# Moving chunk loads, splits and conditioning rows around inside one long transformer kernel

## What is computed

```
sh1, sc1, g1, sh2, sc2, g2 = split(silu(c) @ w_mod + b_mod, 6)      # and the same for c_ctx
hc = modulate(rmsnorm(ctx, norm1_g), csh1, csc1)                    # 256 context tokens
k_c, v_c = context_kv(hc)                                           # columns of w_in
hx = modulate(rmsnorm(x, norm1_g), sh1, sc1)                        # 512 tokens
q, k, v, u, ga, gc = split(hx @ w_in)
y_att  = attend(q, [k, k_c], [v, v_c]) @ w_attn_o
y_conv = silu(layernorm(conv31(a * sigmoid(b)) + conv_b)) @ w_conv_o
x = x + g1 * ((sigmoid(ga) * y_att + sigmoid(gc) * y_conv) @ w_out)
```

## Time and profile before

| | us |
|---|---|
| median of 3 runs | 2408.93 |
| lowest, highest | 2408.12, 2412.94 |
| the profiled execution | 2405.39 |
| its span in the trace | 2403.6 |

### The profile page before, as it was taken

How to read it: one execution, slowest core, us unless ns; L and a number is a source line. 1 busy time by engine, 2 the same in 40 slices (tenths; PEclk the granted TensorE clock), 3 DMA queues, 4 the chain that set the end, 5 groups by cost and what they waited for, 6 DMA issues and landing times.

```text
span 2403.6 us, 29853 instructions
## 1 busy us (share of the span) xinstructions
PE 2179.4 (91%) x10645; PEld 1862.9 (78%) x10645; DVE 1769.7 (74%) x3593; ACT 947.4 (39%) x1543; POOL 1002.4 (42%) x647
## 2 busy tenths in 40 slices
PE   3898899887989999899899999999999979998778
PEld 2686677655768999899788898889888867766557
DVE  7874788876451999999788788887888787444552
ACT  3334555424243444354334333333333343443441
POOL 2441222123434665599644344544455524311111
PEclk8899999988999999999999999999999999977779
DMA  7221111153642454456999999999999943211111
GB/s 290 80 70 66 62 50 70 54 178 130 225 140 82 161 166 149 140 204 235 334 346 376 353 337 332 356 348 344 344 340 359 340 168 101 72 35 35 35 36 44
DMA packets 176946, 455.84 MB, mean 190 GB/s; under 512 B 13600, under 2 KB 80544, under 8 KB 175136
## 3 DMA queue, kind: packets, MB, share of 16 engines
q1 hardware_dynamic: 136720, 293.55, 35.5%
q0 software_dynamic: 36864, 134.23, 14.9%
q10 hardware_dynamic: 3216, 26.15, 2.9%
HBM read 409.84 MB, written 44.04 MB: 189 GB/s over the span
## 4 chain that ended last, share of the span: by engine, by line
PE 63%; DVE 24%; ACT 4%; issue 3%; DMA 2%; POOL 1%; SPq 0%; ACTq 0%; DVEq 0%; POOLq 0%
PE bank L652 12%; PE bank L653 12%; PE bank L654 12%; PE bank L957 7%; PE bank L959 7%; PE bank L961 7%; DVE cout L1850 4%; DVE ohB L2135 4%; PE bank L1027 2%; DVE ohA L2134 2%; PE bank L1056 1%; DVE wk L2036 1%; DVE eqb L2086 1%; PE bank L1039 1%; PE bank L773 1%
## 5 line engine op out<-in xcount | busy, mean ns | idle before, releaser
L1561 POOL TENSOR_TENSOR Rl<-raw,Rh 128x1024 fp32r<-128x1024 f32 x179 | 463.6, 2596 | 831.6 <-ACT Rh L1095 831.2
L652 PE MATMUL bank<-XAh,Rh 128*128 128x384 f32 (+1 forms) x1472 | 534.0, 363 | 36.0 <-POOL Rl L1561 15.3
L1095 ACT ACTIVATE Rh<-raw 128x1024 fp32r<-128x1024 f32 x380 | 400.2, 1057 | 323.9 <-PE bank L961 117.0
L654 PE MATMUL bank<-XAh,Rl 128*128 128x384 f32 (+1 forms) x1472 | 519.7, 353 | 0.0
L653 PE MATMUL bank<-XAl,Rh 128*128 128x384 f32 (+1 forms) x1472 | 519.5, 353 | 0.0
L652 PEld LDWEIGHTS bank<-XAh,Rh 128*128 128x128 f32 x1472 | 278.8, 189 | 59.1 <-issue 20.6
L653 PEld LDWEIGHTS bank<-XAl,Rh 128*128 128x128 f32 x1472 | 279.1, 190 | 17.9
L654 PEld LDWEIGHTS bank<-XAh,Rl 128*128 128x128 f32 x1472 | 278.2, 189 | 18.6
L1607 POOL DMA_INDIRECT ga<-in_v,eid x128 | 196.9, 1538 | 197.5 <-DVE y L2197 178.6
L1607 POOL DMA_INDIRECT ga<-in_un,eid x128 | 172.2, 1345 | 217.3 <-DVE act L2189 193.8
L957 PE MATMUL bank<-Rh,XGh 128*128 128x512 f32 x768 | 238.1, 391 | 5.1 <-issue 5.1
(11 more groups left out here) (272 smaller groups left out, 3411.5 us busy)
## 6 DMA issues: line engine op xcount, KB each, us to landing
raw<-in_u SPq DMA_DIRECT2D x128, 512.0 KB
raw<-in_v SPq DMA_DIRECT2D x128, 512.0 KB
wd<-wb ACTq DMA_DIRECT2D x12, 2048.0 KB, 7.4
wg<-wd SPq DMA_DIRECT2D x30, 768.0 KB
raw<-in_w_mod SPq DMA_DIRECT2D x32, 512.0 KB
raw<-in_w_in SPq DMA_DIRECT2D x32, 512.0 KB
gd<-pk SPq DMA_DIRECT2D x64, 192.0 KB, 1.9
gt<-gd SPq DMA_DIRECT2D x16, 768.0 KB, 10.7
```

Source lines behind the costliest of these rows:

```text
L652: e.matmul(o, sh, mh, start=first, stop=False)
L654: return e.matmul(o, sl, mh, start=False, stop=last)
L1095: e.activation(Rh[:, r % NRING, :], raw[:, n % NRAW, :], ACT.Copy).then_inc(s["hi"], 1)
L1561: e.tensor_tensor(Rl[:, r % NRING, :], raw[:, n % NRAW, :], Rh[:, r % NRING, :].bitcast(F32), ALU.subtract).then_inc(s["lo"], 1)
```

## The change

At the start: the squares of ctx are taken in the middle of `high("hx")`, before block 3, and their products go to the second row of `crow`; SP's last `w_mod` load waits only for the squares of x, and the load of `crow`'s second row waits for all six. ACT and POOL split chunk 8 as well as chunk 7 before they turn to `hc`.

At the merge: SP reads back `sga`, then loads the stream up to chunk 59, and only then reads back `sgc`. ACT splits `w_ao` 2 before the sigmoids of `sga`, and all of `w_ao` 3 to 7 before the squares. PE runs `w_ao` 0 to 5 before the mean (in banks 0, 1, 2, 3, 6, 7), `w_ao` 6 before the variance, 7 after it. DVE puts the products with the gate 0 and 1 among the taps (after 12 and 22), and mod rows 20 and 21 too; rows 22 and 23 go into the scaling loop after its second block, rows 24 and 25 with the bias behind that loop.

```diff
@@ psum_plan
     use(("mu",), 4)
-    use(("ao", 0), 0)
-    use(("ao", 1), 1)
     use(("var",), 5, 1, 0)
-    for cb in range(2, 8):
-        use(("ao", cb), cb % 4)
+    for cb in range(8):
+        use(("ao", cb), (0, 1, 2, 3, 6, 7, 0, 1)[cb])
@@ sync_program
                     if k == 7 and i == 1:
-                        e.wait_ge(s["ssq"], 6)
+                        e.wait_ge(s["ssq"], 4)
...
+            e.wait_ge(s["ssq"], 6)
             e.dma_start(crow[:, 1, :], a["crow"][1].partition_broadcast(128)).then_inc(s["crow1"], 16)
...
-            for v, name, lo in ((sga, "sga", 0), (sgc, "sgc", 8)):
-                if lo == 0:
-                    for i in range(3):
-                        e.wait_ge(s[f"pkg{i}"], 16 * PKG.count(i))
-                    e.wait_ge(free[7], USES["y", 31].done)
-                e.dma_start(v[:, :, :], gg[lo:lo + 8].rearrange("m p t -> p m t")).then_inc(s[name], 16)
+            loads(CH["w_ao", 1] + 1)
+            for i in range(3):
+                e.wait_ge(s[f"pkg{i}"], 16 * PKG.count(i))
+            e.wait_ge(free[7], USES["y", 31].done)
+            e.dma_start(sga[:, :, :], gg[0:8].rearrange("m p t -> p m t")).then_inc(s["sga"], 16)
+            loads(CH["w_ao", 7] + 1)
+            e.dma_start(sgc[:, :, :], gg[8:16].rearrange("m p t -> p m t")).then_inc(s["sgc"], 16)
             loads(CH["w_o", 2])
@@ tensor_program
-            for cb in range(4):
+            for cb in range(6):
                 merge_att(cb)
             o, done = hold(("mu",))
...
-            merge_att(4)
-            merge_att(5)
+            merge_att(6)
             o, _ = hold(("var",))
...
-            merge_att(6)
             merge_att(7)
@@ scalar_program
+                    if name == "hx" and k == 3:
+                        square_sums("ctx", cs, 4, 2, crow[:, 1, :])
...
-            square_sums("ctx", cs, 4, 2)
             high("hx", XA, 0, 512, tmps1, {0: 1, 5: 3})
...
-            ahead(CH["w_qkv", 1, 1] + 2)
+            ahead(CH["w_qkv", 2, 0])
             high("hc", XB, 0, 256, tmps)
...
+            ahead(CH["w_ao", 2])
             e.wait_ge(s["sga"], 16)
             for m in range(8):
                 e.activation(sga[:, m, :], sga[:, m, :], ACT.Sigmoid).then_inc(s["sgas"], 1)
-            ahead(CH["w_ao", 1] + 4)
-            for cb in range(2, 5):
-                ahead(CH["w_ao", cb] + 4)
+            ahead(CH["w_ao", 7])
             for cb in range(8):
                 e.wait_ge(s["sub"], cb + 1)
...
-            ahead(CH["w_ao", 7])
             root("conv", rsd[:, :])
@@ gpsimd_program
             low("hx", XA, 0, 512, tmps1, {1: 1})
-            lows(CH["w_qkv", 1, 1] + 2)
+            lows(CH["w_qkv", 2, 0])
             low("hc", XB, 0, 256, tmps)
@@ vector_program
-            for i in range(2):
+            for i in range(3):
                 modulation(16 + 2 * i, 18 + 2 * i)
-                while n_taps < 7 * 31 + (15, 31)[i]:
+                while n_taps < 7 * 31 + (12, 22, 31)[i]:
                     tap()
-            merge_att(0)
-            modulation(20, 22)
-            merge_att(1)
-            merge_att(2)
+                merge_att(i)
...
             merge_att(3)
-            modulation(22, 24)
-            e.wait_ge(s["wmod"], 8)
-            t_mod = mod_bias(16, 24, 0, n_own)
-            modulation(24, 26)
             merge_att(4)
-            merge_att(5)
             u = USES["var",]
             e.wait_ge(s["ltv"], 8)
             variance("conv", rsd[:, :], bank[u.bank][:, :], D)
+            merge_att(5)
...
+                    if cb == 1:
+                        modulation(22, 24)
                     if cb in (3, 7):
                         merge_att(6 + cb // 4)
+            modulation(24, 26)
+            e.wait_ge(s["wmod"], 8)
+            t_mod = mod_bias(16, 24, 0, n_own)
```

## The result

| | kernel before | changed kernel |
|---|---|---|
| runs | 4 | 4 |
| median us | 2410.40 | 2394.24 |
| lowest, highest | 2408.12, 2412.94 | 2386.53, 2395.22 |
| the profiled execution | 2405.39 | 2386.53 |
| its span | 2403.6 | 2384.7 |

The ratio is 0.9926, with a 95% interval of 0.9902 to 0.995: 12 to 24 us faster, where 18.4 were forecast; the medians differ by 16.2. The two spans differ by 18.9. The profiled execution after is the fastest of its four; the kernel as a whole stands nearer to 2394.

The account below looks back on a forecast made before the run. PE, busy 91% of the span, was taken as the bound, so time is won only where it stands still. 9.1 at the start plus 9.3 at the merge, 18.4 us, gave 2390.5 from 2408.93; range 2385 to 2401.

Parts of the forecast that it names:

- Chunk 8: At the start: PE's 8.07 us wait for chunk 8's low half goes, and the slow clock behind it; gain 9.1 us.
- the 1.4 of slow clock: At the start, from 108 to 113: PE's clock of 0.67 behind the wait goes too, 1.4 us.
- The squares: At the start: squaring ctx before block 3 of hx was booked at nothing, 1.5 us either way.
- Up to the mean: In the merge: DVE's taps end 2.7 us later, but the differences start where they did before.
- the price per split: In the merge: each POOL split that falls among DVE's taps costs DVE 2.0 us.
- Mean to reciprocal: In the merge: one projection before the variance and no row transfer in DVE's way; reciprocal 11.6 us sooner.
- Scaling loop: In the merge, behind the reciprocal: two mod rows added to the loop cost 2.3 us.
- Net of the merge: At the scaling loop's end and PE's start of w_co: 9.3 us gained, bounds 7.5 to 11.3.
- The gate on time: Merge; the rival had w_ao 2 landing late, sigmoids and taps slipping 5.3 us: 2395.8 us, chance 0.14.
- The start's gain is not taken back: Before attention; the rival had ACT's roots and norms take it back, only the merge counting: 2399.6 us, chance 0.09.
- The third: Rival, start and merge: equal waits replace both, at chunk 9 or before the variance; 2408.9 us, chance 0.06.
- The fourth: Rival, w_co 1 to 7: loads behind later mod rows make PE wait before seven chunks; 2413.9 us at least, chance 0.05.

Follow-up runs that it names:

- e4: The changed kernel run again, unedited: 2392.95 us, ratio 0.9935 to the kernel before.
- e3: The kernel before with all of the change's merge edits and none at the start: ratio 0.9964 to the kernel before.
- e5: The kernel before with one line moved, so that ACT splits w_ao 7 ahead of the squares: ratio 0.9967 to the kernel before.
- e7: The changed kernel with sgc read back directly behind sga again, the stream behind both: ratio 0.9941 to the kernel before.
- e2: The kernel before with only the squares of ctx moved before block 3 of hx, and SP's waits with them: ratio 1.0007 to the kernel before.
- e6: The changed kernel with w_ao 7 split behind the squares again: ratio 0.9897 to the kernel before.
- e9: The changed kernel with mod rows 22 to 25 and their bias back in front of the variance: ratio 0.9931 to the kernel before.
- e1: The kernel before with only chunk 8 split right behind chunk 7: ratio 0.9966 to the kernel before.
- e11: The changed kernel with chunks 7, 8 split before ctx's root, ctx squares back, w_ao 7 behind the squares, rows 22 to 25 in the scaling loop's waits: 2382.87 us.

## Why the prediction was right

The forecast of 2390.5 lies 3.7 us under the median of 2394.24, and the interval of the difference takes in its 18.4. The medians differ by 16.2, and by 16.1 in e4.

- **Chunk 8** (9.1): right to the tenth where it stands alone, beside the trace that it was read from. In the changed kernel 6.9 are seen: 0.6 goes to the squares, 1.5 to the clock behind chunk 7's wait. I had looked at the clock behind the wait that goes, and not at the wait one chunk ahead of it, which the profile of before has as well, with 1.28 us. And the 1.4 of slow clock was read from one execution: in three others with that wait it is 1.3 to 1.6 more. Where the clock falls behind chunk 7 on both sides, the first scores come at 203.9 and 204.0 (e3, e5) and at 194.0, some 10 us apart; where it falls on neither, at 200.95 and 192.5 (e4, e7), 8.4 apart.
- **The squares** (0, 1.5 either way): 0.6 us of loss in the stage, within the bounds; not measurable in the time. The reason was the one that the prediction named, POOL's work falling elsewhere among DVE's (e2); only the size was left open.
- **Up to the mean** (taps end 2.7 later, differences unchanged): 2.3 later (44.6 against 42.4 from `sga`'s issue), differences 46.6 against 47.1. The landing of `w_ao` 2, the wait for the gate and the price per split each came out within 0.3. That PE would still wait for the last tap held by only 0.56 us: in e6 the taps come 2.1 sooner, and DVE waits for PE.
- **Mean to reciprocal** (11.6): 11.7 from the first difference on, 12.1 from `sga`'s issue. The size was right, since it was read from both ends: what PE can deliver, and DVE's row from which on it can use it. That moving the rows takes the stall away was right too: e6 has nothing but PE to wait for, with `w_ao` 7 split late. What the prediction did not have is the stall's other half, SP's queue behind `w_ao` 7's split. Without it the rows' place costs 3.2 (e9), and moving that split alone gives 5.4 (e5). By e6 the change did not need the early split, which costs it 1.1. What PE's new order gives by itself was not run alone, so its share in the 11.7 stays open.
- **Scaling loop** (2.3 of loss): 12.1 at the reciprocal, 9.8 to 9.9 at the last scaling, so 2.3.
- **Net of the merge** (9.3): 9.9 in the stage and for PE's first product of `w_co`. Against e1's and e2's stage it is 11.6, just over the prediction's upper bound of 11.3, for the clock of the kernel before is not the same in every execution there either.
- **Rivals.** The gate on time: e7 has it late and costs 5.2. The start's gain is not taken back: DVE still stands 23.79 us before attention. The third: neither wait has an equal in its place (0.44 us ahead of chunk 8, 5.52 for PE ahead of the variance). The fourth, PE waiting 3.3 us before each of seven chunks: 1.70 and 0.81, as before, then none.

Part of the agreement is luck. The profiled spans differ by 18.9, but the change's own stages give 6.9 + 9.9 = 16.8; attention takes 1.7 and the rest gives 3.8, both by where the clock fell. And 9.1 and 9.3 were both read from one execution of the kernel before, whose clock came back early behind the waits for chunk 8 and for the last tap; by e2, e3 and e5 the first part is 1.3 to 1.6 us larger, and by e1 and e2 the merge's is 11.6. That the medians differ by 16.2 all the same, and not by more than 18.4, these single traces do not explain.

## What to carry to other kernels

For each wait for a transfer read the transfer queue as well: what stands ahead of the load in it, and what that waits for. Here a row was late because the load ahead of its own, for another chunk, waited for a split that stood behind eight squares on a third engine, and one moved line took over half of the wait away (9.29 to 3.91). Taking the waiting work out of that place did it as well. Then look again at each such line when the order has changed, since the one that gained 5.4 us before cost 1.1 afterwards. And put filler into the engine's waits, one piece for each, not in front of or behind them.

## What the runs showed of the hardware

**The same wait was followed by either clock.** A wait of 3.2 us in attention was followed by five us at 0.50 in one trace and at 1.00 in another of the same code; such a fall costs 11 of 24 products there, and 1.7 us of the stage. From 108 to 113, about the end of the wait of 8.07 us, the clock was 0.67 in one execution and 0.50 in three. At the start an early fall went with a second one 25 us later and a late fall with none, as told above. Runs of the unedited kernel before lay between 2398.65 and 2416.0 on one chip (29 runs), as wide as the change is large, so single executions tell nothing of parts like these. The Trainium skill (TensorE: Matmul & The Clock Gate, What's actually happening) has the clock fall after idling; the traces agree on the direction, and show that the same idle time can go either way.

**POOL's split holds short instructions of DVE for as long as long ones**, if both inputs lie in SBUF. In e11, beside a POOL split from 548.76 to 551.12 and two from 555.29 to 560.48:

```profile
548.97 2.17 DVE L1702 TENSOR_TENSOR mod<-mod,vecs 128x8 f32<-128x8 f32 x1
...
555.77 2.46 DVE L1971 TENSOR_TENSOR XBl<-sgc,XBh 128x512 fp32r<-128x512 f32 x1 [2.08 <-ACT XBh L1305]
558.15 0.67 DVE L1965 TENSOR_TENSOR sgc<-sgc,bank 128x512 f32<-128x512 f32 x1
558.93 2.10 DVE L1968 TENSOR_TENSOR sgc<-sgc,sga 128x512 f32<-128x512 f32 x1
```

An addition of 8 columns, 0.16 us elsewhere, takes 2.17 and ends at 551.14, with the split. The product with a bank runs through in 0.67 between two that are held. The Trainium skill (SBUF — State Buffer, Who interferes with whom) says just this, that the second SBUF input of a DVE instruction is what meets GpSimd; the trace agrees, and gives the price: about 2 us for a split of 2.4.
